# Late gated one-hots as products of two small factors, two of four groups multiplied out by GpSimd, and a transfer one place earlier on its queue

## What is computed

```python
s1 = einsum('thd,kd->thk', q[:, :, 0], sk[0]);  s2 = einsum('thd,kd->thk', q[:, :, 1], sk[1])
v1, i1 = top_k(s1, 16);  v2, i2 = top_k(s2, 16)
sc, flat = top_k(v1[..., :, None] + v2[..., None, :], 16)
e = i1[flat // 16] * 128 + i2[flat % 16]          # 16 of 16384 experts, for each of 8 heads
g = softmax(sc)
a = gelu(einsum('cd,chkd->chk', x, expert_u[e]))
y = einsum('chk,chkd->cd', g * a, expert_v[e])
```

## Time and profile before

| | us |
|---|---|
| median of three executions | 1538.21 |
| the profiled execution | 1538.31 |
| its span in the profile | 1536.5 |
| TensorE busy | 1461.5 (95%) |
| VectorE busy | 1324.6 (86%) |
| ScalarE busy | 691.0 (45%) |
| GpSimd busy | 782.7 (51%) |

### The profile page before, as it was taken

How to read it: one execution, slowest core, us unless ns; L and a number is a source line. 1 busy time by engine, 2 the same in 40 slices (tenths; PEclk the granted TensorE clock), 3 DMA queues, 4 the chain that set the end, 5 groups by cost and what they waited for, 6 DMA issues and landing times.

```text
span 1536.5 us, 25606 instructions
## 1 busy us (share of the span) xinstructions
PE 1461.5 (95%) x7921; PEld 1254.3 (82%) x7921; DVE 1324.6 (86%) x2653; ACT 691.0 (45%) x1383; POOL 782.7 (51%) x733
## 2 busy tenths in 40 slices
PE   7999999999989868889999999999999999999996
PEld 5777767867578667778999999999999989999985
DVE  5878645346999989798999999999999999999998
ACT  5232456322157657634444444444444444444443
POOL 1000000000059957677767767767767767667662
PEclk9999999999999989999999999999999999999998
DMA  9995111450021165899999999999999999999994
GB/s 344 352 383 194 61 56 56 145 187 1 1 110 51 64 246 232 339 401 402 401 400 401 401 392 403 401 380 400 401 377 402 397 378 402 399 383 401 395 384 161
DMA packets 164992, 448.85 MB, mean 292 GB/s; under 512 B 14683, under 2 KB 50675, under 8 KB 164284
## 3 DMA queue, kind: packets, MB, share of 16 engines
q1 hardware_dynamic: 108732, 243.33, 42.5%
q0 software_dynamic: 56192, 204.66, 33.9%
HBM read 423.72 MB, written 22.32 MB: 290 GB/s over the span
## 4 chain that ended last, share of the span: by engine, by line
PE 75%; DVE 16%; DMA 3%; issue 2%; ACT 2%; POOL 1%; SPq 0%; ACTq 0%; DVEq 0%; POOLq 0%
PE bank L954 15%; PE bank L1225 8%; PE bank L1224 8%; PE bank L1223 8%; PE bank L1246 7%; PE bank L1247 7%; PE bank L1248 7%; PE bank L1239 4%; PE bank L1238 4%; PE bank L1145 2%; PE bank L1058 2%; DMA w_scratch<-staged 1%; PE bank L897 1%; DVE top_i L1959 1%; DVE scores L1960 1%
## 5 line engine op out<-in xcount | busy, mean ns | idle before, releaser
L790 POOL DMA_INDIRECT v_rows<-v_exp,small x192 | 257.4, 1341 | 91.3 <-POOL small L786 51.8
L790 POOL DMA_INDIRECT u_rows<-u_exp,small x192 | 254.3, 1325 | 93.1 <-POOL small L786 52.0
L1223 PE MATMUL bank<-h_hi,u_hi 128*128 128x320 f32 x944 | 291.2, 308 | 0.7 <-ACT staged L1521 0.7
L1225 PE MATMUL bank<-h_hi,u_lo 128*128 128x320 f32 x944 | 291.7, 309 | 0.0
L1224 PE MATMUL bank<-h_lo,u_hi 128*128 128x320 f32 x944 | 291.5, 309 | 0.0
L1246 PE MATMUL bank<-v_hi,g_parts 128*128 128x512 f32 x512 | 200.0, 391 | 0.0
L1247 PE MATMUL bank<-v_lo,g_parts 128*128 128x512 f32 x512 | 199.5, 390 | 0.0
L1248 PE MATMUL bank<-v_hi,g_parts 128*128 128x512 f32 x512 | 199.4, 389 | 0.0
L1624 ACT ACTIVATE v_hi<-v_raw 128x1024 fp32r<-128x1024 f32 x128 | 135.3, 1057 | 117.9 <-PE bank L1248 106.1
L1223 PEld LDWEIGHTS bank<-h_hi,u_hi 128*128 128x128 f32 x944 | 177.2, 188 | 5.4 <-ACT staged L1521 0.9
L1224 PEld LDWEIGHTS bank<-h_lo,u_hi 128*128 128x128 f32 x944 | 177.2, 188 | 4.6
(11 more groups left out here) (257 smaller groups left out, 2965.6 us busy)
## 6 DMA issues: line engine op xcount, KB each, us to landing
v_raw<-v_exp SPq DMA_DIRECT2D x128, 512.0 KB
u_raw<-u_by_key SPq DMA_DIRECT2D x120, 512.0 KB
ada_blk<-ada_w SPq DMA_DIRECT2D x22, 1024.0 KB, 11.1
ring<-w_in SPq DMA_DIRECT2D x18, 1024.0 KB, 10.0
w_row<-w_scratch SPq DMA_DIRECT2D x128, 128.0 KB
w_scratch<-staged SPq DMA_DIRECT2D x2, 4096.0 KB, 17.8
xr<-x SPq DMA_DIRECT2D x8, 512.0 KB, 6.2
ring<-w_branch SPq DMA_DIRECT2D x4, 1024.0 KB, 5.0
```

The source lines that it names most:

```text
L790: pool.indirect_dma_start(out=rows[s], out_offset=None, in_=table, in_offset=bass.IndirectOffsetOnAxis(ap=ix[:, s:s + 1], axis=0))\
L1223: pe.matmul(o, u_hi[:, r, k], h2_hi[:, k], start=(k == 0), stop=False)
L1225: last = pe.matmul(o, u_lo[:, r, k], h2_hi[:, k], start=False, stop=(k == KD - 1))
```

## The change

Each key j of the late tokens is split into a high part (a multiple of 8) and a low part (0 to 7), on GpSimd, before the late loop. In an iteration VectorE compares 16 lanes with the high parts of 16 tokens (`hot_wide`, 256 elements for each partition) and 8 lanes with the low parts (`hot_fine`, 128 elements), and multiplies the gate into `hot_fine`. A group's `hot2` is then one product of 512 elements of the two factors, both spread out by a stride of zero (`gated_rows`). VectorE does the products of r = 0 and 3, GpSimd those of r = 1 and 2; the single-row instructions of both engines are gone. The factor tiles exist once: VectorE waits at the top of an iteration for both of GpSimd's products of the iteration before, and for its own last one.

Besides: `h2_lo` moves from VectorE to GpSimd, ahead of GpSimd's late rows; the late loops of VectorE and GpSimd are cut at m = 16 instead of m = 8; the copy to `h2x` moves ahead of the wait for the early products and of `h2T_kept`; ScalarE waits for `ex_ready` in place of the landed indices, which get a source tile of their own; GpSimd's early rows lose their no-operations; and one semaphore takes the place of two in the long stage.

```diff
-POOL_ROWS = (0, 2, 0, 1)
+WIDE, FINE = 16, 8
+ROUND = 1.5 * FINE * 2.0 ** 23
+LATE_FROM = EARLY * 4
...
+        ex_starts = at("ex_starts", 173.5, [P, P])
...
+        def gated_rows(eng, r):
+
+            four, shape = slice(4 * r, 4 * r + 4), [P, 4, WIDE, FINE]
+            return eng.tensor_tensor(hot2[r].rearrange("p j (a b) -> p j a b", b=FINE),
+                                     hot_wide[:, four].unsqueeze(3).to_broadcast(shape),
+                                     hot_fine[:, four].unsqueeze(2).to_broadcast(shape), ALU.mult)
...
-            sp.wait_ge(a_early_full, N_RUN)
-            sp.dma_start(h2T_kept, h2T[:, :, 0:DS]).then_inc(x_saved, 16)
             sp.wait_ge(scores_read, NT)
             for half in range(2):
                 sp.dma_start(h2x[half * EX:(half + 1) * EX], h2[SPLIT][EX:P]).then_inc(h2x_in, 16)
+            sp.wait_ge(a_early_full, N_RUN)
+            sp.dma_start(h2T_kept, h2T[:, :, 0:DS]).then_inc(x_saved, 16)
...
+            def split_keys(lo, hi):
+
+                keys = picksT[:, 1, lo:hi]
+                high, low = (part[:, lo - LATE_FROM:hi - LATE_FROM] for part in (key_high, key_low))
+                link(pool.tensor_scalar(high, keys, -(FINE - 1) / 2, ROUND, ALU.add, ALU.add))
+                link(pool.tensor_scalar(high, high, -ROUND, 0.0, ALU.add, ALU.add))
+                pool.tensor_tensor(low, keys, high, ALU.subtract).then_inc(keys_split, 1)
...
             stored(pool, ("kT", 1))
+            pool.wait_ge(a_early_full, N_RUN)
+            split_keys(LATE_FROM, 2 * P)
+            pool.wait_ge(h2_hi_done, 1)
+            pool.tensor_tensor(h2_lo, h2T[:, :, 0:DS], h2_hi.bitcast(F32), ALU.subtract).then_inc(h2_lo_done, 1)
 
             def late_rows(lo, hi):
 
                 with pool.Fori(lo, hi) as m:
-                    for n in range(2):
-                        gate_rows(m * 2 + (EARLY // 2 + n), m * 4 + (2 * n + 1), hot2[2 * n + 1], m * 16 + (8 * n + 4),
-                                  range(4 - POOL_ROWS[2 * n + 1], 4))
-
-            late_rows(EARLY // 4, DS_GROUPS // 4)
+                    pool.wait_ge(hot_factors, m * 2 + (2 - EARLY // 2))
+                    pool.nop().then_inc(pool_passed, 1)
+                    for r in (1, 2):
+                        pool.wait_ge(w_full, m * 4 + (r - 3))
+                        pool.nop().then_inc(pool_passed, 1)
+                        gated_rows(pool, r).then_inc(hot2_pool, 1)
+
+            late_rows(EARLY // 4, 2 * DS_GROUPS // 4)
             stored(pool, ("kT", 2))
-            late_rows(DS_GROUPS // 4, ALL_GROUPS // 4)
+            split_keys(2 * P, DS)
+            late_rows(2 * DS_GROUPS // 4, ALL_GROUPS // 4)
...
-                    pe.wait_ge(hots_dve, m * 4 + (q - (EARLY - 1)))
-                    if q % 2 == 1:
-                        pe.wait_ge(hot2_pool, m * 2 + (EARLY // 2 + q // 2 + 1))
+                    pe.wait_ge(hots_dve, m * 4 + (q + 1 + 4 - EARLY))
+                    if q in (1, 2):
+                        pe.wait_ge(hot2_pool, m * 2 + (EARLY // 2 + q))
...
-            act.wait_ge(ex_in, 64)
+            act.wait_ge(ex_ready, 1)
...
             def four_groups(m):
 
-                for r in range(4):
+                def ones(r):
+
                     dve.wait_ge(w_full, m * 4 + (r - 3))
-                    if r < 3:
-                        dve.tensor_tensor(hot1[r], lane.unsqueeze(1).to_broadcast([P, 4, P]),
-                                          picksT[:, 0, bass.ds(m * 16 + 4 * r, 4)].unsqueeze(2).to_broadcast([P, 4, P]),
-                                          ALU.is_equal)
-                    for j in range(4 - POOL_ROWS[r]):
-                        token = bass.ds(m * 16 + (4 * r + j), 1)
-                        ins = dve.tensor_scalar(hot2[r][:, j], lane, picksT[:, 1, token], picksT[:, 2, token],
-                                                ALU.is_equal, ALU.mult)
-                    ins.then_inc(hots_dve, 1)
-
-            with dve.Fori(EARLY // 4, DS_GROUPS // 4) as m:
+                    return dve.tensor_tensor(hot1[r], lane.unsqueeze(1).to_broadcast([P, 4, P]),
+                                             picksT[:, 0, bass.ds(m * 16 + 4 * r, 4)].unsqueeze(2).to_broadcast([P, 4, P]),
+                                             ALU.is_equal)
+
+                dve.wait_ge(hot2_pool, m * 2 + EARLY // 2)
+                dve.wait_ge(hots_dve, m * 4 + (4 - EARLY))
+                at_m = bass.ds(m * 16 - LATE_FROM, 16)
+                dve.tensor_tensor(hot_wide, lane[:, 0:P:FINE].unsqueeze(1).to_broadcast([P, 16, WIDE]),
+                                  key_high[:, at_m].unsqueeze(2).to_broadcast([P, 16, WIDE]), ALU.is_equal)
+                dve.tensor_tensor(hot_fine, lane[:, 0:FINE].unsqueeze(1).to_broadcast([P, 16, FINE]),
+                                  key_low[:, at_m].unsqueeze(2).to_broadcast([P, 16, FINE]), ALU.is_equal)\
+                    .then_inc(hot_factors, 1)
+                ones(0)
+                dve.wait_ge(hot_factors, m * 2 + (1 - EARLY // 2))
+                dve.tensor_tensor(hot_fine, hot_fine, picksT[:, 2, bass.ds(m * 16, 16)].unsqueeze(2)
+                                  .to_broadcast([P, 16, FINE]), ALU.mult).then_inc(hot_factors, 1)
+                ones(1)
+                dve.wait_ge(hot_factors, m * 2 + (2 - EARLY // 2))
+                gated_rows(dve, 0).then_inc(hots_dve, 2)
+                ones(2).then_inc(hots_dve, 1)
+                dve.wait_ge(w_full, m * 4)
+                gated_rows(dve, 3).then_inc(hots_dve, 1)
+
+            dve.nop().then_inc(hots_dve, 4)
+            dve.wait_ge(keys_split, 1)
+            with dve.Fori(EARLY // 4, 2 * DS_GROUPS // 4) as m:
                 four_groups(m)
-            dve.wait_ge(h2_hi_done, 1)
-            dve.tensor_tensor(h2_lo, h2T[:, :, 0:DS], h2_hi.bitcast(F32), ALU.subtract).then_inc(h2_lo_done, 1)
...
-            with dve.Fori(DS_GROUPS // 4, ALL_GROUPS // 4 - 1) as m:
+            dve.wait_ge(keys_split, 2)
+            with dve.Fori(2 * DS_GROUPS // 4, ALL_GROUPS // 4 - 1) as m:
                 four_groups(m)
```

More of the change, by code:

```diff
@@ L420, in build @@
         one = cols(49)
-        four_picks = small[:, 216:224].rearrange("p (a j) -> p a j", a=2)
+        key_high = at("key_high", 10, [P, DS - LATE_FROM])
+        key_low = at("key_low", 11, [P, DS - LATE_FROM])
+        hot_wide = at("hot_wide", 14.5, [P, 16, WIDE])
+        hot_fine = at("hot_fine", 15.5, [P, 16, FINE])
         bs = cols(52, G)
@@ L493, in build @@
                              "hot2_pool", "hots_dve", "apart_done"))
-        w_full, w_staged, picks_copied = sem("w_full"), sem("w_staged"), sem("picks_copied")
+        w_full, w_staged = sem("w_full"), sem("w_staged")
+        keys_split, hot_factors = sem("keys_split"), sem("hot_factors")
         picked, merge_read, own_gelu_done = (
@@ L688, in _ @@
                 rows, cut = slice(half * EX, (half + 1) * EX), slice(half * EX, (half + 1) * EX)
-                sp.dma_start(ex_picks[rows, 0], starts[EX:P, cut]).then_inc(ex_in, 16)
+                sp.dma_start(ex_picks[rows, 0], ex_starts[EX:P, cut]).then_inc(ex_in, 16)
                 sp.dma_start(ex_picks[rows, 1], picks[SPLIT][EX:P, 2, cut]).then_inc(ex_in, 16)
@@ L798, in gather_v, with gate_rows @@
                 gather(n, part, v_exp, v_rows, idx_v, idx_v_set, v_rows_in)
-            def gate_rows(n, g, to, token, some):
-                slots = 2 if len(some) == 4 else 4
-                if not isinstance(g, int) or g >= 2:
-                    pool.wait_ge(w_full, g - (slots - 1))
-                    pool.nop().then_inc(pool_passed, 1)
-                if not isinstance(n, int) or n:
-                    pool.wait_ge(hot2_pool, n)
-                    pool.nop().then_inc(pool_passed, 1)
-                if isinstance(n, int) and n < EARLY:
-                    four = picksT[:, 1:3, token:token + 4]
-                else:
-                    pool.tensor_copy(four_picks, picksT[:, 1:3, bass.ds(token, 4)]).then_inc(picks_copied, 1)
-                    pool.wait_ge(picks_copied, n + (1 - EARLY))
-                    pool.nop().then_inc(pool_passed, 1)
-                    four = four_picks
-                for j in some:
-                    ins = pool.tensor_scalar(to[:, j], lane, four[:, 0, j:j + 1], four[:, 1, j:j + 1],
+            def gate_rows(g):
+                if g >= 2:
+                    pool.wait_ge(w_full, g - 1)
+                if g:
+                    pool.wait_ge(hot2_pool, g)
+                for j in range(4):
+                    token = slice(4 * g + j, 4 * g + j + 1)
+                    ins = pool.tensor_scalar(first_hot2[g % 2][:, j], lane, picksT[:, 1, token], picksT[:, 2, token],
                                              ALU.is_equal, ALU.mult)
                 ins.then_inc(hot2_pool, 1)
+            def split_keys(lo, hi):
[4 more added lines that the diff above has]
```

(7 more changed lines are left out.)

8 lines of the change are left out of this document (4 added, 4 removed).

## The result

The changed kernel takes 1544.44 us in the median of six executions (1542.66 to 1546.54), the kernel before 1537.43 beside it on the same chip (1535.02 to 1539.87): a ratio of 1.0045, with a 95% interval of 1.0035 to 1.0055. That is some 7 us slower; 1546.7 was forecast. The profiled execution took 1544.72, with a span of 1543.0.

A forecast was written before the change was run, and what follows sets the result against it. Two rings of one length, ScalarE with TensorE (5.23) and VectorE (5.24), were taken to bound the late iterations; with added port work, +1.5, +6.9 and 0 gave +8.4 on 1538.31: 1546.7, range 1533.5 to 1557.

The forecast's parts named there:

- all of VectorE's new instructions shut GpSimd out, so the two add up: Late loop: GpSimd stands while VectorE reads two tiles, and VectorE's loop top waits for both products; 6.22 instead of 5.23 us.
- P: Time of one GpSimd product of 512 elements: taken as 1.18 us, twice the mask's 1.155 ns per element; ends 0.59 and 3.18.
- The period: One late iteration: VectorE's 3.86 us plus two GpSimd products, 3.86 + 2 x 1.18 = 6.22, instead of 5.23.
- rival B: Late loop: GpSimd uses VectorE's eight gaps and the drain, saving 0.7 us of each period; no change, 1539.7; chance 0.22.
- Seven periods: Iterations m = 9 to 15, up to the store of the staged gates: 0.99 us more each, +6.9.
- h2_lo and the seam: Start of late loop to m = 8, where engines stopped for the third transposed block: h2_lo 5.9 us on GpSimd; sum +1.5.
- the listed terms 3.7 + 1.0 + 2.4 + 0.6: Iteration m = 8: first gated group, its spread, ScalarE to its second copy, that copy; 7.9 in all, last spread 1.7 later.
- The last four: Last four late iterations: today's 6.44 us, put down to TensorE's next-stage products, is longer than 6.22, so 0 added.
- The second split: Splitting keys at m = 16, 64 elements: covered by the last four iterations, put at nothing; uncovered, 1.3 us.
- A: Late loop: GpSimd reads beside VectorE or P is under 0.72; period 5.23, seam gain of 4.5 stays; 1533.8; chance 0.20.
- C: GpSimd's products cost like today's rows, P = 3.18: period 10.2, h2_lo 15.9; much slower, 1612; chance 0.08.
- The floor of 5.23: Late loop: ScalarE's ring with TensorE takes 5.23 us beside VectorE's own 5.24, so freeing VectorE alone wins about 0.01 per iteration.

The follow-up runs named there:

- VectorE's order: All four products and h2_lo on VectorE, its 512-element comparisons placed between the factor instructions; against the kernel before: 1537.72 us, ratio 0.9994.
- copies: Changed kernel with GpSimd copying the spread-out wide factor to hot2 in place of each of its two products: 1536.93 us, single execution.
- fills: Changed kernel with GpSimd writing zeros of the same size, reading nothing, in place of its two products: 1537.36 us, single execution.
- the two runs with VectorE's order: VectorE's comparisons between factor instructions, all products and h2_lo on VectorE, without and with ScalarE's r = 3 one-hots an iteration ahead: 1537.72 and 1535.24 us.

## Why the prediction was right

**The mechanism.** The step "all of VectorE's new instructions shut GpSimd out, so the two add up" names the right resource, and one, two or no products on GpSimd move the period by 0.27 each. Its direction was half of the truth: the trace before showed only GpSimd standing, and VectorE's comparisons beside GpSimd's rows were no longer than usual (0.675 to 0.682 between 565 and 600 us). After the change mostly VectorE stands (1.56, 5.66). For a period in which the two add up, this makes no difference. The place was wrong, though. The prediction had VectorE waiting at its loop top until both products are done, and took a VectorE that never waits for GpSimd as a sign against it. In the period shown GpSimd's second product ends at 573.02 (570.36 + 2.66), while VectorE reaches its top only at 574.18 and waits 0.16 there for its own last product. The time is lost inside VectorE's instructions, beside the products.

**P.** It was taken as 1.18, between 0.59 and 3.18. The least of the 28 products is 1.171, and with VectorE idle one takes 1.07. Twice the affine select's time for each element was close, some 10% too much. The Trainium skill's figure (GPSIMD Engine Reference, section 3.1: 4497 ns for 2048 elements) gave an estimate of 1.12; the traces show 1.07 alone and 1.17 beside VectorE.

**The period.** 6.22 was forecast, 5.94 measured, and two terms missed in opposite directions. VectorE's own work without GpSimd's products was put at 3.86 and is 4.20: the 256-element comparison has a pitch (the distance to the next start) of 0.54 instead of 0.34 (572.16 to 572.70 with all products on VectorE), and the drain at the loop top is about 0.25 instead of 0.1 (two pitches of 0.60 after 576.11 there end at 577.31, and the next iteration starts at 577.56); no row had given that 0.1. The 0.54 is not a wait for the instruction just before: with VectorE's order an unrelated comparison stands there, and the pitch is still 0.52 to 0.54. This comparison reads every eighth lane number; whether that is the reason was not tested. The products hold VectorE for 2 x 0.88, not 2 x 1.18: some of each lies beside work of VectorE. (The first of the period shown begins at 570.36, 0.18 before the instruction that it holds.) That is 0.6 of each period, near the 0.7 that rival B had; whether GpSimd reads in VectorE's gaps, as B had it, or does its own start and end there, the rows don't tell. So it is in part luck that the time came out within 2.3 us: 0.34 too little and 0.60 too much cancel in part in each period.

**Seven periods.** The sum had +6.9 from the last spread of m = 8 to the store. Measured: 608.73 - 565.53 = 43.20 against 603.22 - 564.26 = 38.96, so +4.2. Seven times 0.71 would be 5.0; the rest is a lead of VectorE, for TensorE still waits for ScalarE at 565.53 and for VectorE only from the next period on. **This is the term that was mis-sized**, by 2.7 us, and it is more than all of the 2.0 us between 1546.7 and the profiled 1544.72. The iterations up to m = 8 add another 0.2 in the same direction; 0.4 in the last four and 0.5 after the start of the long stage, which no row explains, go the other way.

**h2_lo and the seam.** 5.9 was forecast, 6.01 measured; `h2_hi` ends at 539.85 (forecast near 539.9); the last spread of m = 8 at 565.53 (forecast 565.8). The +1.3 (565.53 - 564.26, forecast +1.5) is +2.0 when both traces are set to the end of the picking, as this execution was 0.7 earlier there. The run with `h2_lo` on VectorE shows that the move to GpSimd costs 1.9 of it. The early transfer was counted as a gain that lets `h2_lo` start at 539.9; its worth is 1.6 in the trace of the run that undoes it, and not seen in that run's median. In the sum, the listed terms 3.7 + 1.0 + 2.4 + 0.6 add to 7.7, not 7.9.

**The last four.** They were taken as 0 because 6.44 is more than 6.22: from the store to the long stage it is 25.77 instead of 25.38, +0.4. The second split was not quite covered: VectorE waits 1.05 for it at 605.30. The other parts put at nothing (the early rows, the wait for the indices, the merged semaphore) were not run by themselves.

**The rivals.** A (the floor holds) needed a GpSimd that reads beside VectorE or products under 0.72 us; by its own terms that bound is 0.69, (5.23 - 3.86) / 2. Neither holds: the period is 5.94 with the products, and 5.23 only with copies, with fills or without them. C had P at 3.18 and fell with it. The floor of 5.23 itself was right: it returns in every run in which VectorE needs less (copies, zeros, two products left out, VectorE's order).

## What to carry to other kernels

Before work is moved to an idle engine, ask what both engines read through: here one product moved from VectorE to GpSimd saved VectorE 0.60 us and held it for 0.88, so the idle engine made the busy one slower. Where two rings have the same length, find both before paying for either; a gain of 2.5 us lay in the ring that the change left alone (ScalarE's one-hots an iteration ahead, between the two runs with VectorE's order). Compare small changes over the stretch that they touch, from an event that they don't move.

## What the runs showed of the hardware that was not expected

GpSimd, the slower engine, can hold VectorE for most of the time that GpSimd's instruction runs: 5.66 us for a VectorE instruction of 0.28 beside a 2560-element subtraction, 0.88 more beside a product of 512, 0.41 more beside a copy of 512, nothing beside a fill of 512. A VectorE instruction's duration in a profile may thus be mostly standing; a least duration far below the median (0.675 and 1.134 in the changed kernel's products) is the sign to look for.
